# Query heads of a latent attention: 12 units of 128 columns in place of 16, the rotation by a shuffle on VectorE

## The reference, cut to what matters

```python
q = split_heads(rms_norm(c_q, q_norm) @ w_uq, MLA_HEADS)      # 384 -> 16 x (64 + 32)
q_nope, q_pe = q[..., :MLA_NOPE], q[..., MLA_NOPE:]
x1, x2 = xf[..., 0], xf[..., 1]                               # axial_rope: neighbouring columns
out = jnp.stack([x1 * cos - x2 * sin, x1 * sin + x2 * cos], axis=-1)
q_lat = jnp.concatenate([q_nope, axial_rope(q_pe)], axis=-1)  # against latent keys
q_ctx = jnp.concatenate([q_nope, q_pe], axis=-1)              # against context keys
```

## Time and profile before

| | us |
|---|---|
| median of three runs | 1776.31 |
| lowest and highest run | 1775.35, 1777.21 |
| span of the profiled execution | 1775.4 |
| own time of the profiled execution | 1775.4, its span; the page lists nothing around it |
| query heads, from the first matmul to the first of the key heads | 958.3 to 1004.2 of the span |
| key heads | 1004.2 to 1020.9 |
| values | 1020.9 to 1042.5 |

### The profile page before, as it was taken

How to read it: one execution, slowest core, us unless ns; L and a number is a source line. 1 busy time by engine, 2 the same in 40 slices (tenths; PEclk the granted TensorE clock), 3 DMA queues, 4 the chain that set the end, 5 groups by cost and what they waited for, 6 DMA issues and landing times.

```text
span 1775.4 us, 27067 instructions
## 1 busy us (share of the span) xinstructions
PE 1713.4 (97%) x11006; PEld 1530.3 (86%) x11006; DVE 1068.5 (60%) x1708; ACT 740.2 (42%) x1252; POOL 216.4 (12%) x204
## 2 busy tenths in 40 slices
PE   5999999899999999999999998999999999999997
PEld 3999854699999999999999973334999999999997
DVE  3778666946657787775575645667375653333345
ACT  3433245655643213223345755554466331231333
POOL 0000014422100000000300313333310000000011
PEclk8999998999999999999999988999999999999998
DMA  9555223032465465562311200001244632222231
GB/s 329 160 169 166 78 47 67 20 101 60 120 180 166 142 179 168 152 188 72 90 49 45 87 13 0 1 1 38 82 131 130 201 86 73 83 72 72 82 86 60
DMA packets 255277, 179.45 MB, mean 101 GB/s; under 512 B 12861, under 2 KB 228786, under 8 KB 254130
## 3 DMA queue, kind: packets, MB, share of 16 engines
q1 hardware_dynamic: 255154, 177.72, 34.0%
HBM read 174.15 MB, written 3.62 MB: 100 GB/s over the span
## 4 chain that ended last, share of the span: by engine, by line
PE 86%; DVE 6%; issue 3%; ACT 3%; DMA 1%; POOL 1%; SPq 0%; DVEq 0%; ACTq 0%; POOLq 0%
PE ps L769 22%; PE ps L771 22%; PE ps L770 22%; PE ps L1349 3%; PE ps L1359 2%; DMA ada_a<-in_w_ada 1%; PE ps L948 1%; PE ps L950 1%; PE ps L949 1%; PE ps L825 1%; PE ps L982 1%; DVE w_lo L561 1%; PE ps L1258 1%; PE ps L964 1%; PE ps L835 1%
## 5 line engine op out<-in xcount | busy, mean ns | idle before, releaser
L552 ACT ACTIVATE w_hi<-stage 128x1024 fp32r<-128x1024 f32 (+1 forms) x178 | 186.5, 1050 | 624.4 <-PE ps L771 506.6
L561 DVE TENSOR_TENSOR w_lo<-stage,w_hi 128x1024 fp32r<-128x1024 f32 (+1 forms) x178 | 220.1, 1238 | 287.8 <-ACT w_hi L552 287.6
L769 PE MATMUL ps<-hM_hi,w_lo 128*128 128x320 f32 x952 | 295.3, 310 | 0.0
L771 PE MATMUL ps<-hM_hi,w_hi 128*128 128x320 f32 x952 | 294.2, 309 | 0.0
L770 PE MATMUL ps<-hM_lo,w_hi 128*128 128x320 f32 x952 | 294.1, 309 | 0.0
L769 PE MATMUL ps<-h_hi,w_lo 128*128 128x320 f32 x824 | 255.9, 311 | 2.6 <-DVE h_lo L2438 2.6
L771 PE MATMUL ps<-h_hi,w_hi 128*128 128x320 f32 x824 | 254.6, 309 | 0.0
L770 PE MATMUL ps<-h_lo,w_hi 128*128 128x320 f32 x824 | 254.6, 309 | 0.0
L2650 POOL TENSOR_TENSOR rstd<-rstd,sq 128x320 f32<-128x320 f32 x73 | 77.3, 1066 | 969.1 <-ACT sq L1435 967.6
L769 PEld LDWEIGHTS ps<-hM_hi,w_lo 128*128 128x128 f32 x952 | 178.7, 188 | 3.4 <-issue 3.4
L770 PEld LDWEIGHTS ps<-hM_lo,w_hi 128*128 128x128 f32 x952 | 178.7, 188 | 0.0
(11 more groups left out here) (404 smaller groups left out, 3576.5 us busy)
## 6 DMA issues: line engine op xcount, KB each, us to landing
stage<-in_w_mlp_out SPq DMA_DIRECT2D x83, 512.0 KB, 4.3
stage<-in_w_mlp_in SPq DMA_DIRECT2D x80, 512.0 KB, 4.2
slab_mlp<-in_w_ada SPq DMA_DIRECT2D x28, 1024.0 KB, 5.3
stage<-in_w_in_ac SPq DMA_DIRECT2D x28, 512.0 KB, 3.9
slab_ac<-in_w_ada SPq DMA_DIRECT2D x12, 1024.0 KB, 6.1
ada_a<-in_w_ada SPq DMA_DIRECT2D x8, 1024.0 KB, 16.6
stage<-in_w_out_ac SPq DMA_DIRECT2D x8, 512.0 KB, 4.1
stage<-in_w_out_c SPq DMA_DIRECT2D x8, 512.0 KB, 4.2
```

Source lines behind the costliest of these rows:

```text
L552: nc.scalar.activation(hi_place(n)[:, 0:width], stage[:, n % STAGE, 0:width], ACT.Copy)\
L561: nc.vector.tensor_tensor(lo_place(n)[:, 0:width], stage[:, n % STAGE, 0:width], hi_place(n)[:, 0:width].bitcast(F32), ALU.subtract).then_ ...
L769: mm(out, lo[:, k], xh, start=j == 0, stop=False)
L771: last = mm(out, hi[:, k], xh, start=False, stop=j == k_tiles - 1)
```

## The change

- The query weights are cut into 12 units: 8 plain ones ("n") with the 64 plain columns of two heads each, and 4 positional ones ("p") with the 32 positional columns of four heads each. The exchanged columns are neither loaded nor multiplied. The order is n p n p n p n p n n n n, in 6 pieces.
- SyncE gathers each unit's columns with 3 DMAs (6 a piece, 36 in all, in place of 8).
- ScalarE copies a plain unit in two halves to two heads' rows, and a positional unit as a whole to a tile of its own (`plain_a`, `plain_b`). VectorE shuffles that tile (neighbouring partitions exchanged) into `nt`, multiplies tile and shuffled tile by tables that repeat cosine and sine for four heads (`ropeq`, 8 loads), and adds into `rt` or `rt_b`.
- SyncE moves the rotated and the plain rows of each of four heads to `qm[64:96]` and `qm[96:128]`: 8 DMAs a unit, 32 in all; `qrope_done` counts their landing.
- Two groups of moves stand in SyncE's queue ahead of the key pieces, two behind them. The transposes of the cache rows come after the last query unit, and ScalarE copies them after its last query copy.
- The first value copy on VectorE also waits for `qrope_done`. GpSimd sets the context columns of `ropeq` to 1 and 0. `key_positions` uses `nt` in place of `rt`.

```diff
-          ("in_c", 6, "sweeps", "a"), ("uq", 8, "heads", "ad"), ("uk", 2, "keys", "a"), ("uv", 2, "values", ""),
+          ("in_c", 6, "sweeps", "a"), ("uq", 6, "heads", "a"), ("uk", 2, "keys", "a"), ("uv", 2, "values", ""),
...
+UQ_UNITS = tuple((kind, n) for n in range(4) for kind in "np") + tuple(("n", n) for n in range(4, 8))
...
+SWAP = [c ^ 1 for c in range(ROPE)]
...
+        ropeq, rt_b = lay(77, ("ropeq", [P, 2, T], F32), ("rt_b", [P, 2, T], F32))
+        [plain_a] = lay(55, ("plain_a", [P, 2, T], F32))
+        [plain_b] = lay(103, ("plain_b", [P, 2, T], F32))
...
+        def loads_until(n):
+            uq = range(PIECE_AT["uq"], PIECE_AT["uk"])
+            return sum(2 * KQ if m in uq else 1 for m in range(n % STAGE, n + 1, STAGE))
         def act_split(act, n):
             if n >= PIECE_AT["end"]:
                 return
             width = piece_width(n)
-            act.wait_ge(w_in[n % STAGE], 16 * (n // STAGE + 1))
+            act.wait_ge(w_in[n % STAGE], 16 * loads_until(n))
...
+            def load_queries(j):
+                n = PIECE_AT["uq"] + j
+                sp.wait_ge(w_lo_done, n - STAGE + 1)
+                heads = mats["uq"].rearrange("p k (h c) -> p k h c", c=P)
+                dst = stage[:, n % STAGE, 0:KQ * 2 * P].rearrange("p (k e m) -> p k e m", k=KQ, e=2)
+                for e in range(2):
+                    kind, at = UQ_UNITS[2 * j + e]
+                    for k in range(KQ):
+                        src = heads[:, k, 2 * at:2 * at + 2, 0:64] if kind == "n" else heads[:, k, 4 * at:4 * at + 4, 64:96]
+                        to = dst[:, k, e, :].rearrange("p (h c) -> p h c", c=64 if kind == "n" else ROPE)
+                        load = sp.dma_start(to, src)
+                        load.then_inc(w_in[n % STAGE], 16)
+            def turned_query(g):
+                sp.wait_ge(q_turned, g + 1)
+                for a in range(4):
+                    rows = slice(ROPE * a, ROPE * (a + 1))
+                    sp.dma_start(qm[64:96, 4 * g + a, :], turned_place(g)[rows]).then_inc(qrope_done, 16)
+                    sp.dma_start(qm[96:P, 4 * g + a, :], plain_place(g)[rows]).then_inc(qrope_done, 16)
...
-            sp.dma_start(rope[:, 0:TL], i["c_rope"]).then_inc(mla_in, 16)
+            sp.dma_start(rope[0:64, 0:TL], i["c_rope"][0:64]).then_inc(mla_in, 16)
             load_piece("in_c", dict(PIECES)["in_c"] - 1)
-            load_pieces("uq")
+            for j in range(4):
+                load_queries(j)
+            for s in range(2):
+                for a in range(4):
+                    sp.dma_start(ropeq[ROPE * a:ROPE * (a + 1), s, 0:TL], i["c_rope"][ROPE * s:ROPE * (s + 1)])\
+                        .then_inc(const_in, 16)
+            for j in range(4, 6):
+                load_queries(j)
+            turned_query(0)
+            turned_query(1)
             load_pieces("uk")
+            turned_query(2)
+            turned_query(3)
...
-            for h in range(NH_MLA):
-                ready = (lambda k, j: pe.wait_ge(cn_lo, KQ + k + 1)) if h == 0 else None
-                unit("uq", h, KQ, P, cq_hi, cq_lo, ready=ready, base=P * (h % 2), wide=2 * P)
-                if h == 1:
+            for u in range(len(UQ_UNITS)):
+                ready = (lambda k, j: pe.wait_ge(cn_lo, KQ + k + 1)) if u == 0 else None
+                unit("uq", u, KQ, P, cq_hi, cq_lo, ready=ready, base=P * (u % 2), wide=2 * P)
+                if u == 1:
                     spread_root("ckv", 0)
                     spread_root("ckv", 1)
-                if h == 10:
-                    pe.wait_ge(cn_lo, 2 * KQ + KKV)
-                    for k in range(KKV):
-                        nc.tensor.transpose(ps[:, 6, P * k:P * (k + 1)], ckn[:, k, TL + NP:T + NP], ident[:])
-                    nc.tensor.transpose(ps[:, 7, 0:ROPE], cT[0:ROPE, 5, TL:T], ident[0:ROPE, 0:ROPE])\
-                        .then_inc(tok_t, 1)
+            def tokens_turned():
+                pe.wait_ge(cn_full, 2 * KQ + KKV)
+                for k in range(KKV):
+                    nc.tensor.transpose(ps[:, 6, P * k:P * (k + 1)], ckn[:, k, TL + NP:T + NP], ident[:])
+                nc.tensor.transpose(ps[:, 7, 0:ROPE], cT[0:ROPE, 5, TL:T], ident[0:ROPE, 0:ROPE])\
+                    .then_inc(tok_t, 1)
+            tokens_turned()
             g0, n0 = UNIT_AT["uk"], PIECE_AT["uk"]
+            pe.wait_ge(cn_lo, 2 * KQ + KKV)
...
+            for u, (kind, n) in enumerate(UQ_UNITS):
+                g = UNIT_AT["uq"] + u
+                split("uq", u)
                 act.wait_ge(unit_done, g + 1)
-                if h == 0:
+                if u == 0:
                     act.wait_ge(cn_lo, 2 * KQ)
-                f(two(qm[96:P, h, :]), pair(g, slice(64, 96)), ACT.Copy, scale=MLA_SCALE).then_inc(q_plain, 1)
-                f(two(qm[0:64, h, :]), pair(g, slice(0, 64)), ACT.Copy, scale=MLA_SCALE).then_inc(act_evac, 1)
-                if h in (3, 5):
-                    k = h // 2 - 1
+                if kind == "p":
+                    last = f(two(plain_place(n)), pair(g), ACT.Copy, scale=MLA_SCALE)
+                else:
+                    for e in range(2):
+                        last = f(two(qm[0:64, 2 * n + e, :]), pair(g, slice(64 * e, 64 * e + 64)), ACT.Copy,
+                                 scale=MLA_SCALE)
+                last.then_inc(act_evac, 1)
+                if u in (4, 6):
+                    k = u // 2 - 2
                     act.wait_ge(pc_out, 1)
                     act.wait_ge(cn_full, 2 * KQ + k + 1)
                     f(ck_hi[:, k, :], ckn[:, k, :], ACT.Copy).then_inc(cn_hi, 1)
-                if h == 11:
-                    act.wait_ge(tok_t, 1)
-                    f(tokc[:, 0:256], ps[:, 6, 0:256], ACT.Copy)
-                    f(tokc[:, 256:288], ps[:, 7, 0:ROPE], ACT.Copy).then_inc(tok_out, 1)
-            act.wait_ge(qrope_done, NH_MLA)
+            act.wait_ge(tok_t, 1)
+            f(tokc[:, 0:256], ps[:, 6, 0:256], ACT.Copy)
+            f(tokc[:, 256:288], ps[:, 7, 0:ROPE], ACT.Copy).then_inc(tok_out, 1)
+            act.wait_ge(qrope_done, 32 * NH_MLA)
...
+            def turned_queries(n, g):
+                if n == 0:
+                    dve.wait_ge(const_in, 16 * 9)
+                    dve.wait_ge(km_zero, 3)
+                dve.wait_ge(act_evac, EVAC[g][0])
+                if n >= 2:
+                    dve.wait_ge(cn_full, 2 * KQ + n - 1)
+                to, plain, swapped = turned_place(n), plain_place(n), nt[:, n % 2, :]
+                link(nc.vector.stream_shuffle(swapped, plain, SWAP))
+                tt(to, plain, ropeq[:, 0, :], ALU.mult)
+                link(tt(swapped, swapped, ropeq[:, 1, :], ALU.mult))
+                tt(to, to, swapped, ALU.add).then_inc(q_turned, 1)
+            for u, (kind, n) in enumerate(UQ_UNITS):
+                g = UNIT_AT["uq"] + u
+                if u in (2, 4):
+                    dve.wait_ge(q_turned, u // 2)
+                    key_latents(u // 2 - 1)
+                if u == 8:
+                    dve.wait_ge(q_turned, 4)
                     key_positions()
-                split("uq", h)
-                dve.wait_ge(q_plain, h + 1)
-                if h >= 2:
-                    dve.wait_ge(qrope_done, h - 1)
-                tt(two(rt[64:P, h % 2, :]), pair(g, slice(64, P)), two(rope[64:P, :]), ALU.mult).then_inc(dve_evac, 1)
-                dve.wait_ge(dve_evac, EVAC[g][1])
-                tt(qm[64:96, h, :], rt[64:96, h % 2, :], rt[96:P, h % 2, :], ALU.add).then_inc(qrope_done, 1)
+                split("uq", u)
+                if kind == "p":
+                    turned_queries(n, g)
...
-                    dve.wait_ge(unit_done, UNIT_AT["uq"] + NH_MLA)
+                    dve.wait_ge(unit_done, UNIT_AT["uk"])
+                    dve.wait_ge(qrope_done, 32 * NH_MLA)
```

## The result

The changed kernel takes **1763.23 us** (median of four runs, 1761.37 to 1764.27), the kernel before 1776.61 beside it. The ratio is 0.9923 [0.9911, 0.9935] (in brackets its 95% interval): 0.77% faster. Of the 1776.31 us of before that is 1762.6 us, where 1765.0 was predicted with a range of 1763.0 to 1770.0.

What follows compares the result with a forecast made beforehand. TensorE, busy 97% of the span, was taken as the bound. Key heads 11.6 us earlier less 0.3 us at the value pieces gave 11.3 us: 1776.31 to 1765.0 us, range 1763.0 to 1770.0.

Steps and rivals of the forecast that it cites:

- the sum: Whole kernel: 11.6 us gained in the query heads less 0.3 us lost at the value pieces, 11.3 us in all.
- Four units fewer: Query heads on TensorE: 4 x 2.66 = 10.6 us less; key heads begin 11.6 us earlier, 1.0 of it a stall.
- the groups: VectorE's four rotations of query units (shuffle, two multiplications, addition), foretold to end at 969.7, 976.2, 983.8 and 988.2.
- the bound of 4.7 taken from the reciprocal: Dearest shuffle of 640 columns on VectorE, 4.7 us; key heads then begin 2.5 us later than before: 1778.8, chance 0.06.
- GpSimd's disturbance: Query heads: a VectorE addition slowed beside GpSimd's subtraction, 0.75 us each time, counted twice.
- VectorE's slack: End of query heads: first key piece's split done at 991.6, 1.0 us before its use at 992.6.
- SyncE's queue and the moves: 32 SBUF moves at 0.43 us per issue, last landing at 994.2, costing nothing with 1.0 us to spare.
- the sign that the moves come late: ScalarE's first key copy waits for a DMA; late moves would lose 4.6 us: 1769.6, chance 0.10.
- The rival: Query-weight loads in short runs become the bound, at worst 22.5 us a piece, key heads 10.9 late: 1787.2, chance 0.07.
- The value pieces: Key heads: value loads wait for later token copies, passing on up to 0.5 us; 0.3 taken as lost.
- From there on the order of work is the old one: Everything after the value pieces was taken as unchanged, so no gain or loss was put in there.
- the noise of the runs (0.9 either way): Error term on the whole kernel's time, 0.9 us either way, used in setting the range 1763.0 to 1767.

## Why the mechanism was right, and what the sum left out

**Four units fewer.** Right. The three profiles of the changed kernel have 33.87, 34.74 and 33.49 us of query heads, mean 34.0; the two of before 45.96 and 45.29, mean 45.6. The difference is the 11.6 us of the sum (single pairs give 10.6 to 12.5), and giving the 72 matmuls back took 10.0 of it away again.

**VectorE.** Right in its conclusion. With the 1.8 us by which this execution started later, the groups were foretold to end at 971.5, 978.0, 985.6 and 990.0; they ended at 971.1, 977.7, 985.6 and 989.7. The shuffle took 0.89 us where 0.82 was put in, far from the bound of 4.7 taken from the reciprocal. That the times fit so closely is partly luck, as two errors cancel. GpSimd's disturbance was under-sized: the addition of 983.22 took 2.36 us, 1.5 over its usual 0.82, and a scaling of the key latents at 978.66 took 1.05 in place of 0.49, 2.1 in all and not 2 x 0.75. A split with its group, on the other hand, took 4.2 us and not 4.4. VectorE's slack was to be 1.0 us and was 0.84. The Trainium skill's price for the shuffle ("VectorE: DVE Perf Modes", the perf-mode tier table; 0.75 us as an estimate) was 0.14 under the row.

**SyncE's queue and the moves.** The conclusion was right and one term wrong: a move issues every 0.63 us, not 0.43. The last one landed at 997.1 instead of 996.0 (with the 1.8 us), so ScalarE's first key copy waited for a DMA, which the prediction had named as the sign that the moves come late. They came 1.4 us before TensorE needed them.

**The loads.** The rival fell: a load of 64 KB in short runs landed in 2.1 us in the median, as the load in the earlier trace rows had suggested and the store had not, and halving the runs cost nothing.

**The value pieces.** 0.3 us were taken off and about 0.1 is seen: the key heads are 0.11 us longer, and TensorE's wait for the last key copy is 0.19 us in both kernels. The stretch of the values itself took 39.9 to 42.7 us in the three profiles of the changed kernel, too wide for 0.3 to show.

**What failed.** The step is the sentence that closes the sum, "From there on the order of work is the old one", which puts everything behind the values at nothing. The order is the old one, but 1.2 us at the end of the kernel before came from an instruction block among its last stores, and removing 72 matmuls removed that too. 11.6 - 0.1 + 1.2 = 12.7 us, between the 12.6 and 13.4 us that the two comparisons of medians gave; the prediction had 11.3. With this term in the sum it would have read 1763.6, inside the range. The 1.0 us from there to the 1762.6 measured is within the interval of the ratio (1760.5 to 1764.8), and no run takes it apart; that interval holds the range's end too, so on which side of 1763.0 the value fell was also chance. The range's low end was under-sized as well: of its terms it was mainly "the noise of the runs (0.9 either way)" that pointed down, taken from three runs of before, while 15 runs of it spread over 6.2 us; two profiles of the changed kernel differ by 2.3 us in the scores alone, with TensorE's clock. A slip without effect: a profiled execution's time is not its span. Runs that list both lie 1.8 us over it (1763.56 and 1761.8; 1775.11 and 1773.3), and this cancels in the difference.

## What to carry to other kernels

Where TensorE is busy 97% of the span, matmuls taken from it came back in full, as each unit's other work stayed inside the unit's own time on every engine. Walking the engines' queues once with the rows' durations gave VectorE's margin to two tenths of a microsecond (1.0 foretold, 0.84 measured), partly by errors that cancelled. Price a queue by its issues, not its bytes: 32 small DMAs more cost 19.6 us once the cover was used up. And look at the end of the span for transfers on the "instruction" queues before calling a tail unchanged: it depends on the number of instructions ahead of it.

## What the runs showed of the hardware that was not expected

- An instruction block of 16 KB among stores that fill all 16 DMA engines went with an end about 1.2 us later, in four of the twelve profiles, and in those alone the last store took 4.6 us and not 3.5.
- A move between rows of SBUF held SyncE's queue for 0.63 us, whether it has 640 or 320 columns; the query-weight loads took 0.47 in the median.
- An addition of 128 x 640 on VectorE took 2.36 us beside GpSimd's subtraction of 128 x 768 (2.22 us from 982.68) and 2.37 in the run with doubled shuffles (beside one of 2.13 us from 975.53), 0.82 alone.
- TensorE's granted clock over the same 9.5 us of the first pair of heads was 0.53 to 0.64 in nine of the twelve profiles and 0.82 to 0.85 in three, of the same code: between the two profiles of the unedited changed kernel a difference of 2.3 us in the scores, which a single pair of profiles would put down to the change. What makes it differ stays open.
